# Block one's up-projections: matmul steps in groups, and weights laid out at one distance from the activations per stage

## The reference

```python
def swiglu(x, w_gate, w_up, w_down):
    return (jax.nn.silu(x @ w_gate) * (x @ w_up)) @ w_down

for l in range(DEPTH):                                  # block one
    h = layer_norm(ALPHA * h + 0.5 * swiglu(h, ffn1...), ln1_g[l], ln1_b[l])
    proj = h @ w_in[l]                                  # then three mixers
    ...
    h = layer_norm(ALPHA * h + mix, ln2_g[l], ln2_b[l])
    h = layer_norm(ALPHA * h + 0.5 * swiglu(h, ffn2...), ln3_g[l], ln3_b[l])
```

## Time and profile before

| | us |
|---|---|
| median of 3 runs | 1949.27 |
| lowest, highest | 1947.53, 1949.29 |
| profiled execution, its own time | 1947.75 |
| profiled execution, its span | 1945.9 |
| PE busy in it | 1931.2 |

### The profile page before, as it was taken

The page is one execution under the profiler, slowest core; times in us unless marked ns, Lnnn a source line. Parts: engine busy times, 40 slices in busy tenths (PEclk is TensorE's granted clock), DMA queues, the critical chain, the costliest instruction groups (busy, mean ns, idle before and its releaser), DMA issues.

```text
span 1945.9 us, 42335 instructions
## 1 busy us (share of the span) xinstructions
PE 1931.2 (99%) x16150; PEld 1892.7 (97%) x16150; DVE 1431.5 (74%) x2591; ACT 1019.8 (52%) x1527; POOL 152.7 (8%) x192
## 2 busy tenths in 40 slices
PE   9999999999999999999999999999999999999998
PEld 8999989999999999899999999999999999999998
DVE  6774787987588768879978874667765775667763
ACT  4443687554455447865547443665445444565443
POOL 0001123000100011320010100000000000100000
PEclk9999999999999999999999999999999999999999
DMA  7454433545454544345553665445555555435554
GB/s 265 172 197 170 166 109 112 192 174 193 156 192 172 196 164 145 109 152 194 201 191 140 235 233 183 151 149 185 193 214 177 195 202 208 152 131 195 194 213 154
DMA packets 46830, 346.66 MB, mean 178 GB/s; under 512 B 5344, under 2 KB 6416, under 8 KB 9232
## 3 DMA queue, kind: packets, MB, share of 16 engines
q1 hardware_dynamic: 44416, 335.63, 48.0%
q0 software_dynamic: 2320, 9.74, 1.6%
HBM read 344.29 MB, written 1.07 MB: 177 GB/s over the span
## 4 chain that ended last, share of the span: by engine, by line
PE 91%; DVE 4%; ACT 2%; DVEq 1%; issue 1%; DMA 0%; ACTq 0%; SPq 0%; POOL 0%
PE ps L622 22%; PE ps L623 22%; PE ps L624 22%; PE ps L639 14%; PE ps L630 2%; PE ps L631 2%; PE ps L632 2%; DVE w_lo L1996 1%; PE ps L1162 0%; DVE pj L2465 0%; DMA h<-in_hidden 0%; DVE cst L2486 0%; PE ps L1197 0%; DVE pj L2462 0%; ACT scratch L1669 0%
## 5 line engine op out<-in xcount | busy, mean ns | idle before, releaser
L1996 DVE TENSOR_TENSOR w_lo<-raw,w_hi 128x1024 fp32r<-128x1024 f32 (+1 forms) x582 | 749.3, 1313 | 151.1 <-ACT w_hi L1300 91.5
L622 PE MATMUL ps<-x_hi,w_lo 128*128 128x256 f32 (+3 forms) x2208 | 622.1, 282 | 1.5 <-DVE x_lo L2087 0.6
L624 PE MATMUL ps<-x_hi,w_hi 128*128 128x256 f32 (+3 forms) x2208 | 615.1, 279 | 0.0
L623 PE MATMUL ps<-x_lo,w_hi 128*128 128x256 f32 (+3 forms) x2208 | 614.8, 278 | 0.0
L1297 ACT ACTIVATE w_hi<-raw 128x1024 fp32r<-128x1024 f32 x454 | 466.3, 1052 | 92.5 <-PE ps L639 49.0
L622 PE MATMUL ps<-hid_hi,w_lo 128*128 128x256 f32 (+1 forms) x1536 | 431.5, 281 | 0.1
L624 PE MATMUL ps<-hid_hi,w_hi 128*128 128x256 f32 (+1 forms) x1536 | 430.2, 280 | 0.0
L623 PE MATMUL ps<-hid_lo,w_hi 128*128 128x256 f32 (+1 forms) x1536 | 429.8, 280 | 0.0
L622 PEld LDWEIGHTS ps<-x_hi,w_lo 128*128 128x128 f32 x2208 | 414.9, 188 | 6.4 <-issue 4.2
L623 PEld LDWEIGHTS ps<-x_lo,w_hi 128*128 128x128 f32 x2208 | 415.0, 188 | 0.5
L624 PEld LDWEIGHTS ps<-x_hi,w_hi 128*128 128x128 f32 x2208 | 414.6, 188 | 0.0
(11 more groups left out here) (351 smaller groups left out, 2315.3 us busy)
## 6 DMA issues: line engine op xcount, KB each, us to landing
raw<-in_w_up SPq DMA_DIRECT2D x176, 1024.0 KB, 4.8
raw<-in_w_down SPq DMA_DIRECT2D x64, 1408.0 KB, 6.0
raw<-in_w_in SPq DMA_DIRECT2D x36, 1024.0 KB, 4.8
raw<-in_w_out SPq DMA_DIRECT2D x16, 1024.0 KB, 4.8
cst<-row_copy POOLq DMA_DIRECT2D x2, 1088.0 KB, 8.5
raw<-in_w_up SPq DMA_DIRECT2D x4, 512.0 KB, 7.2
cst<-in_consts POOLq DMA_DIRECT2D x1, 1537.5 KB, 6.5
prm<-in_prm POOLq DMA_DIRECT2D x2, 690.0 KB, 7.2
```

What stands on the lines that cost most here:

```text
L622: mm(dst, low, xa, start=first, stop=False)
L623: mm(dst, high, xb, start=False, stop=False)
L624: return mm(dst, high, xa, start=False, stop=last)
L1996: v.tensor_tensor(dst, src, high.bitcast(F32), ALU.subtract).then_inc(lo_done, 1)
```

## The change

It changes where operands lie and the order of the matmuls in a unit.

- `in_pairs` becomes `in_groups` with a size per width: 4 chunks at 272 columns, 2 at 274, 4 at 258, in every place but `TIGHT`. So the opening's loop, the 258-column loop and the 258-column blocks of the second layer's input projection go in groups of four.
- The places change. The opening gets weights 9 lines apart beside activations 17 lines apart (`x1_hi`, `x1_lo`, now with no room between chunks; before 8 beside 18). The 258-column loop gets 9 beside 17 (before 10 beside 18). The 274-column places keep 10 beside 18 and swap the shifts of high and low weights.
- `three_beside` goes. The last up-projection of block one has 258 columns in all three steps, with low columns in `plain`'s low part; the `tensor_reduce` and its drain become a `tensor_copy` as in the 274-column stages. `plain`'s low part starts right behind the high part at all levels.

```diff
-        PLAIN_LO = [KD * X_PITCH + n * LINE for n in (0, 0, 5, 6)]
-        PLAIN_AT, PLAIN_W = 640, max(PLAIN_LO) + KD * X_PITCH
+        PLAIN_AT, PLAIN_W = 640, 2 * KD * X_PITCH
...
-        x1_hi, x1_lo = chunks(x_hi_all[:, 2 * LINE:], KD, X_PITCH), chunks(x_lo_all, KD, X_PITCH)
+        x1_hi, x1_lo = chunks(x_hi_all, KD, T1), chunks(x_lo_all, KD, T1)
+        cat1_hi, cat1_lo = chunks(x_hi_all[:, 2 * LINE:], KD, X_PITCH), chunks(x_lo_all, KD, X_PITCH)
...
-        BESIDE_LEVEL = 2
+        def plain_of(T):
+            pitch = T1 if T == T2 else X_PITCH
+            return chunks(plain, KD, pitch), chunks(plain[:, KD * pitch:], KD, pitch)
+
+        GROUP = {T1: 4, T1 + 2: 2, T2 + 2: 4}
         Place = namedtuple("Place", "pitch high low")
         TIGHT = Place(P, 0, 0)
-        OPENING = Place(P, LINE, LINE)
-        BESIDE_274 = Place(P + 2 * LINE, 3 * LINE, LINE)
-        LEVEL_274 = Place(P + 2 * LINE, LINE, 3 * LINE)
-        BESIDE_258 = Place(P + 2 * LINE, LINE, 0)
+        OPENING = Place(P + LINE, 2 * LINE, 0)
+        BESIDE_274 = Place(P + 2 * LINE, LINE, 3 * LINE)
+        LEVEL_274 = Place(P + 2 * LINE, 3 * LINE, LINE)
+        BESIDE_258 = Place(P + LINE, 0, 2 * LINE)
...
-            def three_beside(dst, high, low, xa, xb, first, last):
-
-                if first:
-                    mm(dst, high, xa, start=True, stop=False)
-                mm(dst[:, 0:T2 + 2], low, xa[:, 0:T2 + 2], start=False, stop=False)
-                step = mm(dst[:, 0:T2], high, xb[:, 0:T2], start=False, stop=False)
-                return step if first else mm(dst, high, xa, start=False, stop=last)
-
-            def in_pairs(dst, high, low, xa, xb, T):
-
-                for k in range(0, KD, 2):
+            def in_groups(dst, high, low, xa, xb, T, size):
+
+                for k in range(0, KD, size):
                     for w, x in ((low, xa), (high, xb), (high, xa)):
-                        for c in (k, k + 1):
+                        for c in range(k, k + size):
...
-                N = T + 4 if T == T2 else T + 2
-                xs, place = (plain_hi, plain_lo_of(LEVEL_NORM[norm])), level_place(T)
+                N, xs, place = T + 2, plain_of(T), level_place(T)
...
-                    if T == T2:
-                        v.tensor_reduce(wsum[:, 2 * n:2 * n + 2], block[:, T:T + 4].rearrange("p (h c) -> p c h", h=2), AX_X, ALU.add)
-                        dve.drain()
-                        return wsum[:, 2 * n + 1:2 * n + 2]
-                    v.tensor_copy(wcol[:, n:n + 1], block[:, T:T + 1])
-                    return block[:, T + 1:T + 2]
...
+                    v.tensor_copy(wcol[:, 2 * j:2 * j + 1], gate[:, T:T + 1])
```

More of the change, by code:

```diff
@@ L304, in cat1 @@
         def cat1(T):
-            return x_of(T)
+            return (xt_hi, xt_lo) if T == T2 else (cat1_hi, cat1_lo)
         def hid_of(T):
@@ L647, in narrow_unit @@
                 pe.wait_ge(lo_done, turn * 4 + (2 * j + u + 1))
-                if T == T1 + 2 and place is not TIGHT:
-                    last = in_pairs(dst, high, low, xa, xb, T)
+                if T in GROUP and place is not TIGHT:
+                    last = in_groups(dst, high, low, xa, xb, T, GROUP[T])
                 else:
-                    step = three_beside if T == T2 + 4 else three
+                    step = three
                     for k in range(KD):
@@ L667, in first_pair @@
                         high, low = (narrow_at(w, TIGHT, 0, u)[:, k, :] for w in (w_hi, w_lo))
-                        step = three_beside if T == T2 + 4 else three
-                        last = step(ps[:, bank + u, 0:T], high, low, xa[:, k, 0:T], xb[:, k, 0:T],
-                                    n == 0, n == KD - 1)
+                        last = three(ps[:, bank + u, 0:T], high, low, xa[:, k, 0:T], xb[:, k, 0:T],
+                                     n == 0, n == KD - 1)
                         if n == KD - 1:
@@ L745, in crossing_up @@
             def crossing_up(q, turn0, event, norm, T):
[L746 removed]
+                N, xs = T + 2, plain_of(T)
                 pe.wait_ge(up_free, q * NF + (CREDIT - 1))
@@ L1441, in plain_columns @@
             def plain_columns(gain, bias, T):
+                plain_hi, _ = plain_of(T)
                 for n, name in enumerate((bias, gain)):
@@ L1445, in plain_high @@
             def plain_high(gain, k, T):
-                fn(plain_hi[:, k, 0:T], h[:, k, T1 - T:T1], ACT.Identity, scale=plain_par(gain, k)).then_inc(plain_high_done, 1)
+                fn(plain_of(T)[0][:, k, 0:T], h[:, k, T1 - T:T1], ACT.Identity, scale=plain_par(gain, k)).then_inc(plain_high_done, 1)
             def level_square(norm, m, T):
@@ L1511, in pair @@
                     act.wait_ge(gate_ready, q * NF + it * 2 + (j + 1))
-                    fn(silu[:, j, 0:T], silu[:, j, 0:T], ACT.Silu, bias=offset(2 * j, T)).then_inc(silu_done, 1)
+                    fn(silu[:, j, 0:T], silu[:, j, 0:T], ACT.Silu, bias=wcol[:, 2 * j:2 * j + 1]).then_inc(silu_done, 1)
                     if width == W_NARROW:
@@ L2102, in plain_columns @@
             def plain_columns(level, gain, bias, T):
-                plain_lo = plain_lo_of(level)
+                plain_hi, plain_lo = plain_of(T)
                 dve.wait_ge(plain_high_done, level * KD + 1)
@@ L2106, in plain_columns @@
                     c = slice(T + n, T + n + 1)
-                    dst = plain_hi[:, :, T + n + 2:T + n + 3] if level == BESIDE_LEVEL else plain_lo[:, :, c]
-                    v.tensor_tensor(dst, plain_par(name, 0, KD).rearrange("p (k a) -> p k a", a=1),
+                    v.tensor_tensor(plain_lo[:, :, c], plain_par(name, 0, KD).rearrange("p (k a) -> p k a", a=1),
                                     plain_hi[:, :, c].bitcast(F32), ALU.subtract)
             def plain_low(level, gain, k, T):
-                plain_lo = plain_lo_of(level)
+                plain_hi, plain_lo = plain_of(T)
                 dve.wait_ge(plain_high_done, level * KD + (k + 1))
@@ L2174, in level_up @@
                 ha, hb = hid_of(T)
-                def columns(block, n):
-                    if T == T2:
-                        v.tensor_reduce(wsum[:, 2 * n:2 * n + 2], block[:, T:T + 4].rearrange("p (h c) -> p c h", h=2), AX_X, ALU.add)
-                        dve.drain()
-                        return wsum[:, 2 * n + 1:2 * n + 2]
-                    v.tensor_copy(wcol[:, n:n + 1], block[:, T:T + 1])
-                    return block[:, T + 1:T + 2]
                 def pair(it, j, width):
@@ L2187, in pair @@
                     dve.wait_ge(unit_used, turn0 * 4 + it * 4 + (2 * j + 1 + START))
-                    v.scalar_tensor_tensor(out=silu[:, j, 0:T], in0=neg_mean[:, 0:T], scalar=columns(gate, 2 * j),
+                    v.tensor_copy(wcol[:, 2 * j:2 * j + 1], gate[:, T:T + 1])
+                    v.scalar_tensor_tensor(out=silu[:, j, 0:T], in0=neg_mean[:, 0:T], scalar=gate[:, T + 1:T + 2],
                                            in1=gate[:, 0:T], op0=ALU.mult, op1=ALU.add)
@@ L2196, in pair @@
                     dve.wait_ge(unit_used, turn0 * 4 + it * 4 + (2 * j + 2 + START))
-                    v.scalar_tensor_tensor(out=half, in0=neg_mean[:, 0:T], scalar=columns(upb, 2 * j + 1),
+                    v.tensor_copy(wcol[:, 2 * j + 1:2 * j + 2], upb[:, T:T + 1])
+                    v.scalar_tensor_tensor(out=half, in0=neg_mean[:, 0:T], scalar=upb[:, T + 1:T + 2],
                                            in1=upb[:, 0:T], op0=ALU.mult, op1=ALU.add).then_inc(up_free, 1)
@@ L2202, in pair @@
                     dve.wait_ge(silu_done, q * NF + it * 2 + (j + 1))
-                    v.scalar_tensor_tensor(out=half, in0=half, scalar=offset(2 * j + 1, T), in1=silu[:, j, 0:T],
+                    v.scalar_tensor_tensor(out=half, in0=half, scalar=wcol[:, 2 * j + 1:2 * j + 2], in1=silu[:, j, 0:T],
                                            op0=ALU.add, op1=ALU.mult).then_inc(prod_ready, 1)
```

7 lines of the change are left out of this document (1 added, 6 removed).

## The result

The changed kernel takes 1952.40 us in the median (1952.11 to 1952.77, 16 runs), the kernel before 1949.03 us (1946.49 to 1949.44, 16 runs): ratio 1.0022, interval 1.0015 to 1.0029. I had forecast 8.3 us less. The profiled execution has a span of 1950.8 us, 4.9 above that of before.

A forecast was written before the change was run, and what follows sets the result against it. PE was taken to bound the kernel, so only the spacing of matmul starts counts. The terms -1.3 + 0 - 2.6 - 1.7 - 2.2 - 0.5 = -8.3 us, from 1949.27, gave 1941.0 us; range 1930 to 1955 us.

The forecast's parts named there:

- What bounds the kernel: Whole kernel: PE holds 91% of the chain of waits, so time changes only with the spacing of matmul starts.
- 9.2 above its columns: First 274 loop's spacing, 123.3 ns, less its column time; taken as the overhead of loops with one distance.
- Opening: Opening loop, 960 steps: 1.4 ns less a step, -1.3 us; bounds -3.7 and +1.2 us.
- First 274 loop: First loop of 274 columns, 960 steps: already in the better pattern, 0; bounds -2.4 and +2.5 us.
- Second: Second 274 loop, 960 steps: settles as the first does, 126.0 to 123.3 ns, -2.6 us; bounds -4.9 and 0.
- 258 loop: 258-column loop, 960 steps: 116.7 ns for 119.0, -2.2 us; bounds -4.6 and +5.8 us.
- Input projection's blocks: Input projections: 274-column blocks, 624 steps, to 123.3 ns, -1.7 us; 258-column blocks, 144 steps, to 116.7 ns, -0.5 us.
- DVE and the weight writes: 44 sums become copies and 44 drains go; opening writes cost at most 2.2 us more on ACT, 0.6 on DVE; hidden.
- Rival 1: Distance 0 is the bad one: loops slow down, some +4 to +9 us, 1953 to 1958; chance 0.22 at over 0.2%.
- Rival 2: Every stage settles at its floor, 6.7 ns above columns as in block two: -19.7 us, 1929.6; chance 0.13.
- Rival 3: Only the patterns change places; widths and entry make the spacing, not distance: within 3 us of 1949; chance 0.23.
- The rule against the change: Trainium skill: TensorE's read ports never wait and weight loads take no read bandwidth, so no placement matters; sum 0.

The follow-up runs named there:

- part_open: Kernel before, with only the opening's loop given the change's new places and groups of four; 1950.87 us, ratio 1.0012.
- shift1: Changed kernel with all loop weights one line later, so the weights lie 1 line (rest over 4) ahead of the activations; 1957.49 us, ratio 1.0051.
- shift3: Changed kernel with all loop weights three lines later, distance 3 (rest over 4) in place of 0; 1950.30 us, ratio 1.0012.
- shift2: Changed kernel with all loop weights two lines later, distance 2 (rest over 4) in place of 0; 1951.35 us, ratio 1.0021.
- best1: part_258 with its 258 loop's weights moved from distance 0 to distance 3; 1946.11 us, ratio 0.9994 to before.
- wide2: Changed kernel with opening and 258 loop at 18 and 10 lines for 17 and 9, distance 2, 274 places as before; 1949.91 us, ratio 1.0013.
- part_258: Changed kernel with opening and 274 places put back, leaving only the 258-column parts of the change; 1951.78 us, ratio 1.0015 to before.
- wide0: Changed kernel with opening and 258 loop at 18 and 10 lines for 17 and 9, distance 0, 274 places as before; 1949.44 us in one run.
- wide1: Changed kernel with opening and 258 loop at 18 and 10 lines for 17 and 9, distance 1, 274 places as before; 1950.31 us in one run.
- wide3: Changed kernel with opening and 258 loop at 18 and 10 lines for 17 and 9, distance 3, 274 places as before; 1949.57 us, ratio 1.0006.
- best2: Changed kernel with the opening of wide1, the 258 loop of wide0 and the 274 places of before; 1944.36 us, ratio 0.9983 to before.
- best3: Same as best2 but with the opening left as in the kernel before; 1944.62 us, ratio 0.9982 to before.

## Why the prediction was wrong

- **What bounds the kernel** was right. PE holds the chain, the time moved by the spacing in the loops, and stages that the edit leaves alone kept theirs. Of the three signs of being wrong that I had named, two came: a loop that I left at 123.3 ns rose, and the 258 loop stands above 119. The third, new stops in first pairs, left no trace: everything outside the loops and the head moved by about 0.2 us.
- **The step that failed** is "I take that: 9.2 above its columns", the value of the first 274 loop used for every loop with one distance. One distance at all steps is no merit by itself; which distance, and at which width and advance, decides. Measured above the columns: 12.2 ns in the opening, 14.3 in the 258 loop, 11.4 in the 274 loops, in place of 9.2. The 9.2 was also read from a loop at distance 2, while the change puts all of them at distance 0.
- **Opening**: -1.3 forecast, +1.6 to +1.9 us measured (part_open), just outside its upper bound of +1.2.
- **First 274 loop**: 0 forecast, +2.1 against its better pattern (120.54 for 118.40) and -0.4 against the other. **Second**: -2.6 forecast, -0.4 measured. That both would settle alike was right, at 125.6 ns and not at 123.3. What I missed is that at the old distance the first loop has one pattern or the other from execution to execution: on the upper level of before, where its median lies, both loops are at 120.97. So I put a sum that was worked out on an execution with the first loop at 118.40 onto a median that has it at 120.97, and the offset of 1.5 us that I took between the two was part of this.
- **258 loop**: -2.2 forecast, +2.7 measured, the largest miss. The row was there: the 258-column step beside a load at distance 0 was the dearest of its loop, on average 121 ns; all steps now take 121.8. I kept that as a bound and chose another stage's value for the same width.
- **Input projection's blocks**: -1.7 and -0.5 us forecast. The 274-column blocks did not move. Their high-high form:

```profile
L627 PE MATMUL ps<-x_hi,w_hi 128*128 128x274 f32 x208 | 43.1, 289 | 0.0
```

  stands at 289 ns as before. In the 258-column blocks that form has 281 ns for 283, some 0.3 us in 144 steps if spacing follows duration. Going from distance 2 to 0, which lengthened the first 274 loop, did nothing to the 274 blocks.
- **DVE and the weight writes** were hidden as said. DVE in the 258 window is busy 96.23 us for 99.64, and the copies wait for PE for 5.6 us where the sums had 0.5:

```profile
865.00:975.00 110.00, 96.23 (x196) 1.00 0.52 188
```

```profile
L2176 DVE COPY small<-ps 128x1 f32<-128x1 f32 x19 | 2.9, 155 | 5.6 <-PE ps L627 5.6
```

- **The rivals.** Rival 1, slower, came true in sign and by its own test (258 loop above 121 ns), but its price, +4 to +9 us, took every loop at its worst; +3.4 was just below, and +5.7 against the lower level inside it. Its mechanism, "distance 0 is the bad one", is wrong as a general statement: with two lines of advance distance 0 is the best place for 258 columns. Rival 2 fell: no changed loop came near 6.7 ns above its columns. Rival 3 had the two patterns right, but not that the distance does nothing: shift1 to shift3 refute that. My upper end of 1955 did hold the time, by the width that rival 1 gave it; the forecast itself had the wrong sign.
- **The rule against the change.** shift1 to shift3 move nothing but where the weights lie, and a 274 loop goes from 120.5 to 122.7, 118.4 and 121.6 us. The Trainium skill, in TensorE: Matmul & The Clock Gate, on what happens when a matmul is issued, has the two reads independent, and I had read it as saying that no placement matters. Here placement matters, and the measurement decides. That it is the two reads that hinder each other is not shown by any run.

What stays open: why the pair of distance and advance acts as it does, and which other property parts groups from the old order at the same distance. The runs give spacings, no mechanism. The writes of ACT and DVE move along with the weights in every one of them, so their part, if they have one, is not told apart either. How a 274 loop comes into one of its two patterns wasn't settled either: the first loop had the better one in the profiles of before, part_open, shift2, best1 and wide2, and the worse one in part_258, wide0, wide1, wide3, best2 and best3; the second loop had the worse one in all of them.

## What to carry to other kernels

Where PE is busy throughout, read the spacing of its starts by stage and how far it lies above the columns, and don't carry the value of one width or stride to another: shift one operand by a line at a time at each of them and measure. Look at the list of times, not at the median alone: two levels hide a gain or a loss of their own size, and a profile shows only one of them.

## What the runs showed of the hardware that was not expected

At a granted clock of 1.00 (2.4 GHz) throughout, moving only the weights by 64 bytes at a time changed the spacing of 258-column matmuls from 121.8 to 118.5 ns, and of 274-column ones between 123.3 and 127.8. At distance 0, putting weights and activations one 64-byte line further apart from chunk to chunk (10 and 18 lines for 9 and 17) changed the spacing at 258 columns from 121.8 to 116.9 ns. The same 960 matmuls of 274 columns at the same distance ran in 118.40 or 120.97 us, in eleven profiles within 0.01 us of one of the two, the first loop in either and the second always in the longer, and this goes with the two levels of the whole kernel, 2.6 us apart.
